# Last expert's high and low sums: turned with the identity and added by VectorE

## The reference, cut to what matters

```python
def moe_swiglu(h, w_router, w_gate_up, w_down):
    t = h.reshape(-1, D)
    logits = (t @ w_router).astype(F32)
    top_val, top_idx = lax.top_k(logits, TOP_K)
    top_w = jax.nn.softmax(top_val, axis=-1)
    combine = jnp.sum(jax.nn.one_hot(top_idx, N_EXPERTS, dtype=F32) * top_w[..., None], axis=1)
    out = jnp.zeros_like(t)
    for e in range(N_EXPERTS):
        gt, up = jnp.split(t @ w_gate_up[e], 2, axis=-1)
        y = (jax.nn.silu(gt) * up) @ w_down[e]
        out = out + combine[:, e:e + 1].astype(t.dtype) * y
    return out.reshape(B, S, D)
```

## Time and profile before

| | us |
|---|---|
| median of 3 runs | 3087.06 |
| lowest and highest run | 3083.06, 3090.32 |
| the profiled execution | 3082.03 |
| its span, first to last instruction | 3080.3 |
| gate and up of rank 0 and the eighth, with their folds | 655 to 852 of the span |

### The profile page before, as it was taken

How to read it: one execution, slowest core, us unless ns; L and a number is a source line. 1 busy time by engine, 2 the same in 40 slices (tenths; PEclk the granted TensorE clock), 3 DMA queues, 4 the chain that set the end, 5 groups by cost and what they waited for, 6 DMA issues and landing times. The chain is left out here.

```text
span 3080.3 us, 42961 instructions
## 1 busy us (share of the span) xinstructions
PE 2982.0 (97%) x17865; PEld 2610.1 (85%) x17865; DVE 2006.8 (65%) x2232; ACT 1518.7 (49%) x1698; POOL 24.0 (1%) x41
## 2 busy tenths in 40 slices
PE   6999999999999999999999999999999999999998
PEld 6889897788888888977888888998798798996898
DVE  4548646666656555757898897555555756787755
ACT  4543344355545444646777775433434445533453
POOL 0001000000000000000000000000000000000000
PEclk9999999999999999999999999999999999999999
DMA  5438641077757655768999997541444143445142
GB/s 193 137 107 271 237 165 56 9 292 280 261 191 249 231 190 178 240 221 298 358 360 351 354 364 276 181 151 50 152 164 164 42 164 137 155 150 166 59 168 96
DMA packets 197852, 606.10 MB, mean 197 GB/s; under 512 B 19648, under 2 KB 59401, under 8 KB 154394
## 3 DMA queue, kind: packets, MB, share of 16 engines
q1 hardware_dynamic: 192306, 588.23, 54.1%
q0 software_dynamic: 3872, 12.71, 1.3%
q10 hardware_dynamic: 1480, 2.41, 0.3%
HBM read 602.26 MB, written 1.05 MB: 196 GB/s over the span
## 5 line engine op out<-in xcount | busy, mean ns | idle before, releaser
L2331 DVE TENSOR_TENSOR w_lo<-ring,w_hi 128x2048 fp32r<-128x2048 f32 x304 | 696.0, 2292 | 273.3 <-ACT w_hi L2155 269.6
L358 DVE TENSOR_TENSOR w_lo<-ring,w_hi 128x2048 fp32r<-128x2048 f32 (+2 forms) x209 | 469.3, 2247 | 473.0 <-ACT w_hi L349 472.4
L2155 ACT ACTIVATE w_hi<-ring 128x2048 fp32r<-128x2048 f32 x304 | 581.1, 1915 | 322.9 <-PE ps L2017 147.2
L349 ACT ACTIVATE w_hi<-ring 128x2048 fp32r<-128x2048 f32 (+2 forms) x209 | 392.8, 1881 | 637.5 <-PE ps L472 480.8
L472 PE MATMUL ps<-h_hi,w_hi 128*128 128x256 f32 x1616 | 404.8, 288 | 8.0 <-PEq L171 4.5
L472 PE MATMUL ps<-h_lo,w_hi 128*128 128x256 f32 x1616 | 400.0, 284 | 0.0
L472 PEld LDWEIGHTS ps<-h_hi,w_hi 128*128 128x128 f32 x1616 | 312.0, 193 | 12.5 <-issue 8.0
L472 PEld LDWEIGHTS ps<-h_lo,w_hi 128*128 128x128 f32 x1616 | 312.2, 193 | 0.3
L472 PE MATMUL ps<-h_hi,w_lo 128*128 128x256 f32 x1616 | 228.4, 284 | 0.9 <-DVE w_lo L358 0.7
L2011 PE MATMUL ps<-w_hi,h_hi 128*128 128x512 f32 x560 | 222.0, 396 | 2.0 <-DVE arena L2384 1.7
L2011 PE MATMUL ps<-w_hi,h_lo 128*128 128x512 f32 x560 | 218.5, 390 | 0.0
(11 more groups left out here) (586 smaller groups left out, 5662.8 us busy)
## 6 DMA issues: line engine op xcount, KB each, us to landing
ring<-in_moe_w_gate_up SPq DMA_DIRECT2D x224, 1024.0 KB, 5.0
ring<-in_moe_w_down SPq DMA_DIRECT2D x112, 1024.0 KB, 4.9
ring<-in_w_in SPq DMA_DIRECT2D x58, 1024.0 KB, 6.9
ring<-in_w_in_even SPq DMA_DIRECT2D x30, 1024.0 KB, 6.8
ring<-in_dense_w_gate_up SPq DMA_DIRECT2D x22, 1024.0 KB, 7.8
ring<-in_w_in_odd SPq DMA_DIRECT2D x16, 1024.0 KB, 7.1
arena<-in_w_ada POOLq DMA_DIRECT2D x24, 512.0 KB, 4.7
ring<-in_b_w_in SPq DMA_DIRECT2D x12, 1024.0 KB, 6.3
```

Of the source, the lines that this page charges most:

```text
L349: k.nc.scalar.activation(self.part(k.w_hi, b, m), src, ACT.Copy).then_inc(k.hi_ready, 1)
L358: k.nc.vector.tensor_tensor(self.part(k.w_lo, b, m), src, self.part(k.w_hi, b, m).bitcast(F32), ALU.subtract).then_inc(k.lo_ready, 1)
L2155: nc.scalar.activation(high(g, h), raw(g, h), ACT.Copy).then_inc(k.hi_ready, 1)
L2331: nc.vector.tensor_tensor(low(g, h), raw(g, h), high(g, h).bitcast(F32), ALU.subtract).then_inc(k.lo_ready, 1)
```

## The change

PE now turns the 128 x 128 blocks of the sums with the identity (`nc.tensor.transpose`), four per panel, so PSUM holds 4 blocks of 128 columns in place of 64. A new step on DVE, `eighth_fold`, adds columns n and n + 64 of each block in one `tensor_reduce` from PSUM into `v.eighth_folded` in SBUF. `eighth_silu` (ACT) and `eighth_product` (DVE) read that tile. `eighth_silu` waits for DVE's `eighth_added` where it waited for PE's `folded`. `eighth_product` moves behind `eighth_sums` where a panel of the eighth is under way. `v.fold` and the instruction that made it go.

```diff
-    v.fold = a(18176, 1, EIGHTH_ROOM)[:, 0, :]
+    v.eighth_folded = [a(8448 + 256 * i, 4, EIGHTH_ROOM) for i in range(2)]
...
             def fold_rows(c):
                 pe.wait_ge(product_ready, unit(EIGHTH, c, 0) + 1)
-                if c == 0:
-                    pe.wait_ge(fold_made, 1)
                 if c >= 2:
-                    pe.wait_ge(eighth_ready, c - 1)
+                    pe.wait_ge(eighth_added, c - 1)
                 for j in range(4):
-                    at = slice(j * EIGHTH_ROOM, (j + 1) * EIGHTH_ROOM)
-                    last = nc.tensor.matmul(k.ps[:, 4 + c % 2, at], v.eighth_sums[c % 2][:, j * P:(j + 1) * P],
-                                            v.fold, start=True, stop=True)
+                    at = slice(j * P, (j + 1) * P)
+                    last = nc.tensor.transpose(k.ps[:, 4 + c % 2, at], v.eighth_sums[c % 2][:, at], k.ident[:, :])
                 last.then_inc(folded, 1)
...
             def eighth_silu(c):
-                act.wait_ge(folded, c + 1)
+                act.wait_ge(eighth_added, c + 1)
                 if c >= 2:
                     act.wait_ge(eighth_ready, c - 1)
-                nc.scalar.activation(v.eighth_gated[c % 2], k.ps[:, 4 + c % 2, 0:2 * EIGHTH_ROOM],
-                                     ACT.Silu).then_inc(eighth_gated, 1)
+                nc.scalar.activation(v.eighth_gated[c % 2],
+                                     v.eighth_folded[c % 2][:, 0:2, :].rearrange("p c n -> p (c n)"), ACT.Silu).then_inc(eighth_gated, 1)
...
+            def eighth_fold(c):
+                dve.wait_ge(folded, c + 1)
+                if c >= 2:
+                    dve.wait_ge(eighth_ready, c - 1)
+                rows = k.ps[:, 4 + c % 2, :].rearrange("p (j h n) -> p j n h", j=4, h=2)
+                nc.vector.tensor_reduce(v.eighth_folded[c % 2], rows, AX_X, ALU.add).then_inc(eighth_added, 1)
+
             def eighth_product(c):
                 dve.wait_ge(eighth_gated, c + 1)
                 nc.vector.tensor_tensor(v.eighth_hidden[:, 2 * c:2 * c + 2, :].rearrange("p c n -> p (c n)"),
-                                        v.eighth_gated[c % 2], k.ps[:, 4 + c % 2, 2 * EIGHTH_ROOM:4 * EIGHTH_ROOM],
+                                        v.eighth_gated[c % 2],
+                                        v.eighth_folded[c % 2][:, 2:4, :].rearrange("p c n -> p (c n)"),
                                         ALU.mult).then_inc(eighth_ready, 1)
...
-            nc.vector.tensor_tensor(v.fold, k.ident[:, 0:EIGHTH_ROOM], k.ident[:, EIGHTH_ROOM:P],
-                                    ALU.add).then_inc(fold_made, 1)
...
                     if waiting:
                         (e0, c0, g0), waiting = waiting, None
                         product(e0, c0)
-                        for n in folds_at(g0):
-                            eighth_product(n)
+                        made = folds_at(g0)
+                        for n in made:
+                            eighth_fold(n)
                     split(g + 1, 1)
                     if c < GATE_PANELS:
                         eighth_sums(c)
+                    while made:
+                        eighth_product(made.pop(0))
                     continue
...
                     product(e, c)
                 if e == 1 and c == DOWN_PANELS:
                     y_parts(EIGHTH)
+                for n in folds_at(g):
+                    eighth_fold(n)
                 split(g + 1, 1)
```

More of the change, by code:

```diff
@@ L1857, in routed_experts @@
         folded, eighth_gated, eighth_ready = st.sem("folded"), st.sem("eighth_gated"), st.sem("eighth_ready")
-        eighth_high, eighth_split, fold_made = st.sem("eighth_high"), st.sem("eighth_split"), st.sem("fold_made")
+        eighth_high, eighth_split, eighth_added = st.sem("eighth_high"), st.sem("eighth_split"), st.sem("eighth_added")
         def fills(e):
@@ L2507, in _ @@
                 split(0, h)
-            waiting = None
+            waiting, made = None, []
             for g, (e, c) in enumerate(order[0:whole_end]):
```

## The result

The changed kernel takes 3090.9 us (median of 8 runs, 3089.29 to 3093.46) against 3084.12 for the kernel before in the same series (8 runs, 3079.34 to 3090.32). The ratio is 1.0023, 95% interval 1.0013 to 1.0032: slower by 7 us, between 4 and 10. The forecast was +3.6 us on 3087.06, so 3090.7. The time agrees with it, but the difference is twice as large. The traces say why both hold: the stretch in which the change lies became 3.0 us longer, about as the sum had it, and some 7 us were lost 1300 us later, in a part of the kernel that the change does not touch. That the two times lie so near is luck: the forecast difference is half of the measured one, and the runs of before came out 3 us lower than those that the forecast stood on.

A forecast was written before the change was run, and what follows sets the result against it. PE, 97% busy, was taken as bound but waiting on an ACT and DVE chain for rank 0's products; +5.44 - 1.46 - 0.37 = +3.6 us on 3087.06 gave 3090.7 us, range 3084.5 to 3096.0.

The forecast's parts named there:

- The bound and the chain of the products: Between rank 0's panels PE waits on a chain over ACT and DVE of about 4.8 us, limiting what shorter folds gain.
- The nine waits of 0.2 us: PE's waits before L2011 at seven places with one eighth panel and two with two, read as waits for rank 0's products.
- the single stretches: Seven places with one panel of the eighth between two of rank 0; PE's wait grows 0.20 to 0.57, gain 0.
- After (0,12): Last fold, followed at once by a panel of rank 0 with no chain to wait for: -0.37 us.
- The double folds: Two folds together after (0,2) and (0,6): of 0.83 us saved on PE 0.73 arrives, twice, -1.46 us.
- The two places: After (0,1) and (0,5), two eighth panels together: DVE's new step delays split and low part 2.72 us each, +5.44.
- rival C: DVE's strided reduction is dear: at 2.0 us each, +8.2 us in all, 3095.3 us; chance 0.05.
- The cover: Slack before PE wants the delayed second-half split: 2.4 us with one eighth panel, 1.6 us where two folds stand together; cost 0.
- Rival D: PE's turns are no cheaper than the products, a fold taking 1.09 us: +7.4 us, 3094.5 us; chance 0.05.
- The rest: Moved eighth_product, SBUF reads by silu and product, dropped v.fold instruction, ring loads up to 3 us later: taken as 0.
- something else: Any outcome other than the forecast and its four rivals; chance 0.03.
- the things named as what would make the forecast wrong: Low part not last ready, PE waits at other second halves, clock falling after two longer waits, DMA last releasing a split.

The follow-up runs named there:

- the turns alone: The kernel before with PE turning the sums, silu and product reading PSUM directly, DVE's addition left out: 3088.12 us, ratio 1.0017.
- the dearer addition: The changed kernel with a second DVE reduction of 1.21 us ahead of each addition, its result unused: one run, 3097.83 us.
- filled up: The changed kernel with four identity turns after each fold, restoring PE's old instruction count: 3086.66 us, ratio 1.0010.
- the later silu: The changed kernel with ACT issuing the next panel's second-half split ahead of eighth_silu: 3090.19 us, 1.0025; with 54 identity turns added, 3083.61 us, 0.9994.

## Why the prediction was right, and where it was not

**The bound and the chain of the products: right.** The nine waits of 0.2 us were for rank 0's products. They took up what PE saved in the single stretches, with the change and with the turns alone. The forecast put them at 0.57 us and they are 0.67 to 0.69. The term mis-sized is the fold: I took 0.81 us to 0.44 from PE's rows. The waits stand in front of weight loads, and counted there a fold took 0.89 (698.85 to 699.74 in the trace of before) and takes 0.43 to 0.44 now, so 0.45 less and not 0.37. Where the cover is complete that changes nothing. After (0,12), where nothing covers it, the gain was 0.45 and not 0.37.

**The double folds: right.** -0.72 us for each by the start of the next panel's loads, -0.73 forecast, and PE then waits 0.25 and 0.22 us, as it must if the products bound it. By that panel's loads of the low part it is -0.82 and -0.77.

**The two places: right in mechanism, 0.17 us too dear.** 2.55 us each and not 2.72. The split follows the silu's start by 0.21 us, where I took 0.36 from a silu that read PSUM; that is 0.15 of it. The reduction took 0.684 us, 0.69 forecast: rival C's condition did not come about, and a strided read of 512 elements cost what the contiguous one of the earlier trace rows costs.

**The cover: right.** In single stretches and after the double folds PE did not wait at the second half of a panel; the dearer addition found the edge behind the double folds: with 1.73 us for each (the next one's begin against this one's), the line of rival C gives a split at 692.6 against 692.1, a wait of 0.5, and 0.56 was measured.

**Rival D: refuted.** The record of a turn is 273 ns, and four take 0.43 us from start to start (660.65 to 661.08). The Trainium skill, page "TensorE: Matmul & The Clock Gate", section "Part 4: PE-mode transpose", gives about 275 ns for one turn; the traces here agree with that as the length of a record, and not as what each of four in a row costs.

**The sum of the stretch:** 2 x 2.55 - 2 x 0.72 - 0.45 = +3.2, and +3.1 with 0.82 and 0.77 for the double folds; measured +3.0 between its two ends, forecast +3.6.

**The step that failed** is "The rest", put at 0, where the runs show +7.3 us. I went through the buffers, the ring and `v.fold`, and ended that paragraph at 0, without asking what else a kernel with 112 instructions fewer on PE does differently. The trace of before had what was needed to ask it: the page's row of 142 instruction packets, 16.4 KB each, and at 2165 us a split that waits 1.70 us for a DMA with PE close behind. It did not have the price, for no row showed what happens if the two meet. The Trainium skill, page "Runtime: NRT & Kernel Launch", section "Instruction fetch mechanics", says that the instruction memory is refilled in blocks of 16 KiB, each of 256 instructions, and that crossing such a boundary is "mostly hidden". The traces agree with the block (16.4 KB, some 252 records of PE) and show no price where nothing waits: from 1440 to 2040 us before and after keep their distance to 0.03 us, although their packets fall on different transfers. Where one falls on a transfer that PE's next work waits for, the jump of 5.9 to 7.5 us stands beside it. The range held the time because scatter and rivals had made it wide, not because this case was in it; what happened is the "something else" that had 0.03. Of the things named as what would make the forecast wrong, none came true as written: the clock stayed at 1.00 after the two longer waits, and the split that ends a wait for a DMA at 2165 us did so before the change too. A fall of the clock and a wait for a DMA are what cost the time all the same, at a place that the text did not have in mind.

**What stays open.** The sum by the traces, +3.0 in the stretch and +7.3 in the jump, is 10.3; the medians give 7.1 with an interval of 4.0 to 9.9 (0.0013 to 0.0032 of 3084). Single executions differ by some us in where else the clock falls, so the last 3 us can't be assigned from traces.

## What to carry to other kernels

Cost an edit in the stretch where it lies by asking what PE waits for now: waits of 0.2 us were enough here to say that time saved on PE would not arrive, and a queue in which a short step stands ahead of a long split turned that step's new wait into a stall. Then ask what the edit does to the length of the program: here 112 instructions moved the loading of code onto a transfer that the kernel waits for, 1300 us behind the edit, and that cost more than the edit itself. So read the difference of two traces at several fixed instructions along the span before putting a measured difference down to the edit, and try the same edit with the old program length restored.

## What the runs showed of the hardware that was not expected

- Code arrives while the kernel runs, in packets of 16.4 KB (142 of them, 2.33 MB), and shares the DMA engines with the weights; a second instruction queue brings 52 packets of 8 KB, none of them within that second transfer in these traces. Kernels that differ by 112 or 144 instructions on PE, far ahead of that moment, have the large ones some 11 to 15 us earlier or later. A 1 MB transfer that took 7.3 to 7.5 us without such a packet took 8.6 to 8.9 with one, at the two places compared.
- Two kernels with the same useful arithmetic differ by about 4 to 7 us (the changed order, filled up or not) and 9 to 10 us (the later silu), and the one with 108 or 112 idle instructions more is the faster.
- A stall of PE is not priced by its length alone. Waits of 1.33 and 1.57 us close together left the granted clock at 1.00 over the next stretch; 2.45 and 1.56 us were followed by 0.83 at one place and 0.66 at the other; and 1.84 us before L1276, where 0.68 had left it at 1.00, was followed by 0.69 over 22 us.
- A reduction over pairs that lie 64 apart in PSUM, 512 elements for each partition, takes 0.684 us, as long as a copy of 512 elements from PSUM in the same stretch (0.68).
